# Grouped 32-column matmuls for router logits, layer-norm sums and step sizes, and turned sums moved between the last gate and up pieces

## What is computed

```python
# layer 0
z, xbc, dt, u, v = split(rmsnorm(x) @ W_in)          # 1024, 2048, 16, 1024, 1024 columns
xbc = silu(causal_conv4(xbc)); dt = softplus(dt + bias)
y = ssd(xbc, dt)                                     # 16 heads, state 64 x 128 per head
y = group_rmsnorm(y * silu(z))
g = gelu(u) * mix(layernorm(gelu(v)))                # spatial gating, chunks of 128 rows
x += concat(y, g) @ W_out;  x += swiglu(rmsnorm(x))  # D_FF = 2816
# layer 1
x += conformer_conv(rmsnorm(x))                      # GLU, 31-tap depthwise conv, layernorm, silu
logits = rmsnorm(x) @ router                         # 8 experts, the two largest are used
x += sum over the two experts e of gate_e * swiglu_e(rmsnorm(x))
return rmsnorm(x), new states
```

## Time and profile before

| | us |
|---|---|
| median of 3 runs | 1371.74 (1371.33 to 1373.18) |
| the profiled execution, its own time | 1371.72 |
| its span | 1370.0 |
| TensorE busy (matmul) | 1327.5, 97% of the span, 7031 instructions |
| VectorE (DVE) busy | 372.4, 27% |
| ScalarE (ACT) busy | 171.4, 13% |
| GpSimd (POOL) busy | 61.4, 4% |
| mean granted TensorE clock | 0.989 |
| DMA | 381.51 MB, mean 278 GB/s |

### The profile page before, as it was taken

One profiled execution on the slowest core, in us unless ns is written; L12 is line 12 of the kernel. 1 busy time (PEld: TensorE's weight loads), 2 busy tenths in 40 slices (PEclk: granted clock), 3 DMA queues, 4 the chain that ended last, 5 costly groups with the idle time before them and its releaser, 6 DMA issues.

```text
span 1370.0 us, 16556 instructions
## 1 busy us (share of the span) xinstructions
PE 1327.5 (97%) x7031; PEld 808.9 (59%) x7031; DVE 372.4 (27%) x829; ACT 171.4 (13%) x352; POOL 61.4 (4%) x87
## 2 busy tenths in 40 slices
PE   7999999999999999989999999999999999999887
PEld 6888888888888888858633335444333333333323
DVE  3535885421111115943310111100102011011011
ACT  1241423010000101032200000000000000000002
POOL 2003210000000202000000000000000000000000
PEclk9999999999999999999999999999999999999999
DMA  8537722565455433383799999996999999999994
GB/s 264 214 126 257 251 93 93 185 175 161 135 186 179 146 123 123 109 289 129 278 353 354 411 418 401 413 361 264 409 409 404 418 411 403 385 402 418 398 417 174
DMA packets 136155, 381.51 MB, mean 278 GB/s; under 512 B 6892, under 2 KB 62748, under 8 KB 129882
## 3 DMA queue, kind: packets, MB, share of 16 engines
q1 hardware_dynamic: 128339, 360.03, 69.7%
q0 software_dynamic: 3216, 11.54, 2.6%
q10 hardware_dynamic: 4530, 8.91, 2.0%
HBM read 372.54 MB, written 9.01 MB: 279 GB/s over the span
## 4 chain that ended last, share of the span: by engine, by line
PE 87%; DVE 5%; DMA 4%; SPq 1%; issue 1%; ACT 1%; DVEq 0%; ACTq 0%
PE ps L1730 30%; PE ps L2210 15%; PE ps L2281 13%; PE ps L2229 8%; PE ps L2241 4%; DVE both L1417 3%; PE ps L1956 3%; PE ps L2292 2%; DMA both<-in_moe_w_down_dram 2%; DMA both<-in_moe_w_gate_dram 2%; PE ps L2153 1%; PE ps L2258 1%; DMA both<-in_w_in_even_dram 1%; PE ps L1739 1%; PE ps L1948 1%; PE ps L2019 1%
## 5 line engine op out<-in xcount | busy, mean ns | idle before, releaser
L1730 PE MATMUL ps<-both 128*128 128x264 f32 x2080 | 472.4, 389 | 5.0 <-ACT both L978 3.7
L1730 PEld LDWEIGHTS ps<-both 128*128 128x128 f32 x2080 | 396.9, 192 | 75.1 <-issue 5.1
L2210 PE MATMUL ps<-both 128*64 128x512 f32 (+3 forms) x960 | 235.6, 563 | 8.3 <-DMA both<-in_moe_w_gate_dram 4.9
L2281 PE MATMUL ps<-both 128*64 128x512 f32 (+1 forms) x704 | 178.4, 597 | 1.9 <-DMA both<-in_moe_w_down_dram 1.9
L2210 PEld LDWEIGHTS ps<-both 128*64 128x64 f32 (+1 forms) x960 | 89.9, 148 | 137.9 <-issue 119.5
L2229 PE MATMUL ps<-both 128*64 128x512 f32 (+1 forms) x576 | 117.8, 560 | 0.9 <-ACT both L1007 0.9
L2281 PEld LDWEIGHTS ps<-both 128*64 128x64 f32 (+1 forms) x704 | 58.0, 143 | 101.8 <-issue 100.2
L2229 PEld LDWEIGHTS ps<-both 128*64 128x64 f32 x576 | 41.3, 137 | 68.4 <-issue 67.1
L1638 DVE TENSOR_TENSOR both<-both,ps 128x512 f32<-128x512 f32 (+1 forms) x18 | 16.7, 942 | 209.9 <-PE ps L2210 209.9
L2241 PE MATMUL ps<-both 128*32 128x512 f32 (+1 forms) x576 | 60.4, 560 | 0.0
L1627 DVE TENSOR_TENSOR both<-both,ps 128x512 f32<-128x512 f32 (+1 forms) x9 | 8.9, 987 | 132.6 <-PE ps L2229 132.6
(11 more groups left out here) (362 smaller groups left out, 904.4 us busy)
## 6 DMA issues: line engine op xcount, KB each, us to landing
both<-in_moe_w_up_dram SPq DMA_DIRECT2D x32, 2048.0 KB
both<-in_moe_w_gate_dram SPq DMA_DIRECT2D x32, 2048.0 KB
both<-in_moe_w_down_dram SPq DMA_DIRECT2D x32, 2048.0 KB
both<-in_moe_w_gate_dram SPq DMA_DIRECT2D x16, 1536.0 KB
both<-in_moe_w_down_dram SPq DMA_DIRECT2D x16, 1536.0 KB
both<-in_moe_w_up_dram SPq DMA_DIRECT2D x16, 1536.0 KB
both<-in_w_in_even_dram SPq DMA_DIRECT2D x10, 2048.0 KB
both<-in_ffn_w_gate_dram SPq DMA_DIRECT2D x11, 1024.0 KB
```

Of the source, the lines that this page charges most:

```text
L1730: ins = mm(ps[:, 0:T], w[:, c, cols:cols + P], src[:, c, :], start=c == 0, stop=c == nk - 1)
L2210: ins = mm(out, xg[:, 4 * j + c, 0:cap], w[:, c, r, :], start=j + c == 0, stop=j + c == 4)
L2281: ins = mm(out, lhsT, w[:, b - b0, 512 * h:512 * (h + 1)], start=b + r == 0, stop=b + r == 11)
```

## The change

Stationary blocks of 32 columns, put at output partitions 0, 32, 64 and 96 in turn (chunk c goes to group c mod 4), take the place of full-width ones, so that a tile holds four partial sums in its four quarters. A second, small matmul with stacked identities (mask32, 32 columns, each the sum of four identity blocks) or with ones joins the quarters.

- Step sizes: 8 grouped matmuls (tile dtp), copied by ScalarE into GV's first chunk, and, behind the turned conv rows, 3 joining matmuls into dt. Zeroed tails are added to wdt and wrt, as the last chunk's block reaches past them.
- The sample block moves from behind v3 to behind v1; ScalarE's copies and store with it, the broadcasts from behind v4's activation to behind v2's. dtT is no longer copied by ScalarE but multiplied by DVE into a block-diagonal matrix (dtown), and one matmul with odd spreads it. The matrices odd, own and mask32 are made by three reductions on DVE behind the x copies.
- Layer-norm sums of layer 0: `stat_part` (8 grouped) where `stat` was, a copy on ScalarE scaled by 1/32, `stat_joined` (1 matmul) one tile later; the root of the variance moves behind u5.
- Router logits: chunks 0 to 3 behind w2_5, 4 to 7 behind the norm's two sums; DVE copies tile lgp to SBUF; 3 joining matmuls behind three turned row groups.
- The last expert: (0,0), (0,1), (2,0) of the turned sums go between the pieces of `up(2, 10)`, (1,0) and (1,1) stay between those of `down(1, 14)`.

```diff
 psum_tiles
-    add("dt", ("dt_raw", 2))
+    add("dtp", ("dtp_ready", 1))
     for i in range(4):
         add(("crow", i), ("crow_ready", i + 1))
+    add("dt", ("dt_raw", 2))
     for c in range(DC):
         add(("v", c), ("gv_ready", c + 1))
-        if c == 3:
+        if c == 1:
...
         if i == 0:
-            add("lg", ("lg_ready", 2))
+            add("lgp", ("lgp_read", 1))
+    add("lg", ("lg_ready", 2))
 GpSimd
             then(g.memset(ident[:, :], 0.0))
+            then(g.memset(wdt[:, DC * 16:DC * 16 + 16], 0.0))
+            then(g.memset(wrt[:, DC * EXP:DC * EXP + 24], 0.0))
 ScalarE
+                if c == XBC:
+                    filled(act, "dtp")
+                    a.activation(dtp, tile("dtp")[:, 0:T], ACT.Copy).then_inc(sem("dtp_ready"), 1)
...
-                if c == 4:
+                if c == 2:
                     for k in range(4):
                         sample_bc(k)
-                if c == 3:
+                if c == 1:
...
-                    filled(act, "dtT")
-                    a.activation(dts[0:HEADS, :], tile("dtT")[0:HEADS, 0:16], ACT.Copy).then_inc(sem("dtT_ready"), 1)
...
+                if k in (1, 4):
+                    part = ("lnv_mean_part", "lnv_var_part")[k // 4]
+                    act.wait_ge(sem("stat_full"), STATS.index(part) + 1)
+                    a.activation(SQ1[:, 0, :], STAT[:, 0:T], ACT.Copy, scale=1.0 / 32).then_inc(sem("stat_read"), 1)
...
-                if k == 4:
+                if k == 5:
                     load_root_table()
                     root("lnv_var", 1)
 DVE
+            dve.wait_ge(sem("ident_ready"), 1)
+            then(v.tensor_reduce(mask32, ident[:, :].rearrange("p (d m) -> p m d", d=4), AX.X, ALU.add))
+            dve.wait_ge(sem("esel_ready"), 1)
+            then(v.tensor_reduce(odd, esel.rearrange("h c m -> h m c"), AX.X, ALU.add))
+            then(v.tensor_reduce(own, esel, AX.X, ALU.max))
...
+            filled(dve, "dtT")
+            v.tensor_tensor(dtown, bc(tile("dtT")[0:HEADS, 0:16], 1, [HEADS, DC, 16]), bc(own, 2, [HEADS, DC, 16]),
+                            ALU.mult).then_inc(sem("dtT_ready"), 1)
...
+            filled(dve, "lgp")
+            v.tensor_copy(lgs, tile("lgp")[:, 0:T]).then_inc(sem("lgp_read"), 1)
 TensorE
+            def stat_part(name, ready, SQ):
+
+                pe.wait_ge(sem("stat_read"), STATS.index(name))
+                for c in range(DC):
+                    g = 32 * (c % 4)
+                    pe.wait_ge(sem(ready), c + 1)
+                    ins = mm(STAT[g:g + 32, 0:T], ones[:, 0:32], SQ[:, c, :], start=c < 4, stop=c >= 4)
+                ins.then_inc(sem("stat_full"), 1)
+
+            def stat_joined(name, part):
+
+                pe.wait_ge(sem("stat_read"), STATS.index(name))
+                mm(STAT[:, 0:T], ones[:, :], part, start=True, stop=True).then_inc(sem("stat_full"), 1)
...
-            for k in range(BLK):
-                n = ROWS[k]
-                for c in range(DC):
-                    ins = mm(ps[0:n, 16 * k:16 * k + 16], H[:, c, P * k:P * k + n], wd[:, c, :], start=c == 0,
-                             stop=c == DC - 1)
+            for c in range(DC):
+                g = 32 * (c % 4)
+                ins = mm(ps[g:g + 32, 0:T], wdt[:, 16 * c:16 * c + 32], H[:, c, :], start=c < 4, stop=c >= 4)
...
+            pe.wait_ge(sem("dtp_ready"), 1)
+            ps = claim("dt")
+            for k in range(BLK):
+                n = ROWS[k]
+                ins = mm(ps[0:n, 16 * k:16 * k + 16], dtp[:, P * k:P * k + n], mask32[:, 0:HEADS], start=True,
+                         stop=True)
+            done(ins)
...
-                if s == 0:
+                    if s + j != 1 or s:
+                        continue
                     pe.wait_ge(sem("xc_ready"), XBC + 1)
...
-                    for c in range(DC):
-                        ins = mm(ps[:, 16 * c:16 * c + 16], esel[:, c, :], dts[0:HEADS, :], start=True, stop=True)
-                    done(ins)
+                    done(mm(ps[:, 0:P], odd, scr(10368, P)[0:HEADS, :], start=True, stop=True))
...
                     if s == 0 and j == 1:
-                        for c in range(DC):
-                            stat("lnv_mean", "gv_ready", 0, GV, c)
+                        stat_part("lnv_mean_part", "gv_ready", GV)
+                    if s == 0 and j == 2:
+                        stat_joined("lnv_mean", SQ1[:, 0, :])
                     if s == 1 and j == 0:
-                        for c in range(DC):
-                            stat("lnv_var", "vsq_ready", 0, SQ1, c)
+                        stat_part("lnv_var_part", "vsq_ready", SQ1)
+                    if s == 1 and j == 1:
+                        stat_joined("lnv_var", SQ1[:, 0, :])
...
 logits(c)
-                    pe.wait_ge(sem("lg_zero"), 1)
-                    mm(lg[:, 0:24], ident[:, :], L, start=True, stop=False)
                 pe.wait_ge(sem("h_ready"), 4 * DC + c + 1)
-                for k in (0, 1, 2) if c < DC - 1 else (1, 2, 0):
-                    n = ROWS[k]
-                    ins = mm(lg[0:n, 8 * k:8 * k + 8], H[:, c, P * k:P * k + n], wr[:, c, :], start=False,
-                             stop=k == 0 and c == DC - 1)
-                return ins
+                g = 32 * (c % 4)
+                return mm(lgp[g:g + 32, 0:T], wrt[:, EXP * c:EXP * c + 32], H[:, c, :], start=c < 4, stop=c >= 4)
...
-                    for c in range(3) if 4 * s + j == 3 else range(4 * s + j - 1, 4 * s + j) if 4 * s + j > 3 else ():
-                        logits(c)
+                    if 4 * s + j == 5:
+                        for c in range(4):
+                            logits(c)
...
-            ins = logits(DC - 1)
+            for c in range(4, DC):
+                ins = logits(c)
...
+            pe.wait_ge(sem("lgp_read"), 1)
+            ps = claim("lg")
+            for k in range(BLK):
+                n = ROWS[k]
+                ins = mm(ps[0:n, 8 * k:8 * k + 8], lgs[:, P * k:P * k + n], mask32[:, 0:EXP], start=True, stop=True)
+            done(ins)
...
 up(k, n, ...)
-                            if between and j + m == 0:
-                                between()
+                            if between:
+                                between(2 * j + m)
...
-                up(2, 10, 1, (lambda: scatter_block(3)) if s else None)
+                def between_up(i):
+
+                    if i == 0 and s:
+                        scatter_block(3)
+                    if s == STATIC and i == 1:
+                        pe.wait_ge(sem("moe_mul"), t * XMULS + (first + 2 * reps))
+                        pe.wait_ge(sem("t_free4"), t * STEP4 + (USES[s]["scat"][0] + SCAT))
+                        pe.wait_ge(sem("t_free5"), t * STEP5 + (USES[s]["scat"][1] + SCAT))
+                    if s == STATIC and i:
+                        sum_rows(*((0, 0), (0, 1), (2, 0))[i - 1])
...
                     if s == STATIC:
-                        if r == 1:
-                            pe.wait_ge(sem("t_free4"), t * STEP4 + (USES[s]["scat"][0] + SCAT))
-                            pe.wait_ge(sem("t_free5"), t * STEP5 + (USES[s]["scat"][1] + SCAT))
-                            for h in range(2):
-                                sum_rows(0, h)
-                        else:
-                            for h in range(2):
-                                sum_rows(1, h)
-                            sum_rows(2, 0)
-
+                        sum_rows(1, r - 1)
+
+                up(2, 10, 1, between_up)
                 down(1, 14, between_down)
```

More of the change, by code:

```diff
@@ L284, in build @@
         SQ0 = GV
+        dtp = GV[:, 0, :]
         st = reg(10608, 4096).rearrange("p (b c n) -> p b c n", b=4, c=DC)
@@ L326, in build @@
         SQ1 = scr(7168, DC * T).rearrange("p (c t) -> p c t", c=DC)
+        odd = scr(10240, P)[0:HEADS, :]
+        dtown = scr(10368, P)[0:HEADS, :].rearrange("h (c j) -> h c j", c=DC)
+        own = scr(10496, DC)[0:HEADS, :]
         esel = scr(11264, 1024)[0:HEADS, :].rearrange("h (c m) -> h c m", c=DC)
@@ L371, in build @@
         ysb = reg(11776, 1024)
+        lgs = ysb[:, 0:T]
         xg = reg(12800, 1024).rearrange("p (c j) -> p c j", c=DC)
@@ L472, in wview @@
             return ring[:, 4096 * slot:4096 * (slot + 1)] if n < NSM else ring[:, 6144 * slot:6144 * (slot + 1)]
-        wdt = sb("wdt", DC * 16)
-        wrt = sb("wrt", DC * EXP)
+        wdt = sb("wdt", DC * 16 + 16)
+        wrt = sb("wrt", DC * EXP + 24)
         bc = lambda ap, axis, shape: ap.unsqueeze(axis).broadcast_to(shape)
@@ L2029, in _ @@
                 stat("lnc_var", "csq_ready", 0, SQ2, c)
-            wr = wrt[:, :].rearrange("p (c n) -> p c n", c=DC)
-            lg = tile("lg")
+            lgp = tile("lgp")
             def logits(c):
                 if c == 0:
-                    for sname, value in TILES[NUM["lg"] - RING][1]:
+                    for sname, value in TILES[NUM["lgp"] - RING][1]:
```

(14 more changed lines are left out.)

10 lines of the change are left out of this document (4 added, 6 removed).

## The result

The changed kernel takes 1364.61 us (median of 4 runs, 1363.96 to 1366.13), the kernel before 1372.46 beside it (1371.33 to 1373.52): 0.9941 of its time, 95% interval 0.9925 to 0.9956. It is faster, inside the range, but 5.1 us over the forecast: 7.9 us were gained, not 12.2. The execution profiled took 1364.55 us, span 1362.8.

A forecast was written before the change was run, and what follows sets the result against it. TensorE, busy nearly the whole span, was taken to bound the kernel, with the chain on it wherever the change touches. Gains of 7.0, 2.3 and 2.9 sum to 12.2 us: 1371.7 - 12.2 = 1359.5 us, range 1356.0 to 1365.0.

The forecast's parts named there:

- Prices: On TensorE: a grouped block of eight 264-column matmuls costs 1.13 us instead of 3.56, of four 0.66, a join 0.445.
- the taps' row: Profile row of the conv taps in four column groups: 32 matmuls in 3.59 us, used to price the grouped blocks.
- Rival 4: Column groups don't overlap with one shared moving operand: each block of eight costs 3.56 us, total 1369.3; chance 0.04.
- Step sizes and the sample block: Ahead of the second v block: it starts at 98.0 us instead of 102.5, gain 4.5, whether the clock falls or not.
- Rival 1: Sample chain starts late, DVE only 4.5 us earlier; TensorE waits 2 to 3 before the variance: 1361.5 to 1362; chance 0.12.
- The two sums: Layer-norm mean and variance sums: 1.98 us less each on TensorE; spatial mix 7.0 us earlier, bounds 5.1 to 8.5.
- this chain is late next: Variance root, DVE's scaling of v and the running sums hold the spatial mix: gain 7.0 us instead of 8.5.
- Start additions: DVE's three reductions (some 2.7 us) and two tiny memsets fit DVE's idle stretch at the start: no cost.
- Router logits: Grouped logits between the last w2 tiles and the positions: 2.3 us gained before the experts, bounds 0.6 to 3.6.
- rival 2: The clock falls once or twice more in the new waits, 1.7 us per fall: 1361.2 to 1363; chance 0.15.
- Turned sums: Last expert: 12 turning matmuls move between gate and up pieces, hidden in DMA waits: 2.9 us gained, bounds 1.2 to 3.1.
- Rival 5: Weight stream from 1100 to 1339 us sets the end; at a rate 5.1% lower the 12.2 us are gone; chance 0.02.

## Why the prediction was right, and where it failed

**Prices.** Right in sum: a grouped block of eight took 1.10 us in each place. From start to start, with what the full-width tile behind it takes over 3.56, that is 1.14 for the mean's sum (127.61 to 128.64, then 3.67 to 132.31), forecast 1.13; the join 0.44 (132.31 to 132.75), forecast 0.445; the logits' first four 0.69 (633.12 to 640.93 less two tiles), forecast 0.66. The sum was right by some luck: the block itself took 1.03 where the taps' row gave 0.93, and the change of form and back 0.11 where the forecast had 0.2. The rule of the Trainium skill that was weighed ("TensorE: Matmul & The Clock Gate", "Measured speedup vs the span model", 2.38 times for three tiles) would have made each block 0.2 longer, by an estimate from its figure. Its rate gives 1.11 for the block, the taps' 0.93, and the 1.03 measured lies between; the taps' row with the forecast's 0.2 came nearer for block and change together. Rival 4, no overlap, is out.

**Step sizes and the sample block.** Right: second v block at 98.93, that is 98.0 and the 1.0 of the late end of xbc. The clock held between 86 and 92 (1.00 where it was 0.72), and by the wait for the decay that was worth nothing, as forecast. Rival 1 did not come: DVE took the mean at 133.02, having waited 1.11 us for the join, and TensorE does not wait before the variance.

**The two sums.** Right in size and in cause. From the end of xbc to the mix 6.7 and 6.6 us, forecast 7.0, and "this chain is late next" is what the run with the whole variance sum shows: DVE's scaling of v holds the mix, and the second of the two splits is worth 0.4 us of its 1.98.

**Start additions.** Put at nothing, and no cost shows: at the end of xbc the nine profiles with them are 0.2 us earlier in the mean than the four without, with a scatter of over 2 us in either group.

**Router logits.** This is the step that failed: "2.3 us in front of the experts", with bounds 0.6 to 3.6, measured at -1.8. Its times up to the clock's fall were right: the last w2 tile 9.0 us earlier by the profile (5.4 carried and 3.6 its own); the logits in DVE at 644.97 against 652.79, 5.4 + 2.4 where 2.3 was forecast; and the fifth row turn waited for ScalarE, as said. What it had wrong is the price of that wait. The wait was 2.08 us long at the end of a chain of very small matmuls, and the clock fell in it. The forecast had priced such a fall at 1.7 us, from 6 us of mixed work in the earlier trace rows, and put it in rival 2 with 0.15; in the sum it stood at nothing. The clock was low for nearly 14 us, over the last row turns, the positions and most of the gather: the stretch got 1.8 us longer instead of 2.3 shorter, and the first expert's first piece came 3.6 us earlier instead of 9.3.

By the spans 5.0 us are missing (7.2 for 12.2): 4.1 here, 1.0 by the late end of xbc, 0.3 between there and the mix and 0.4 between mix and w2, less 0.7 more than forecast in the last expert, rounded. Three things show that most of the 4.1 went to the clock: the logits of before bring the stretch back to 52.5; the five idle matmuls cut it by 5.3 us (6.9 of the whole by medians); and with all waits filled the same edit gives 1.8 us in the stretch and 2.2 in the whole. Not all of the 5.3 is the change's own, since filling the waits of the kernel before gives 1.6 in the same stretch. The change's own loss to the clock is therefore 3.7 us, or 3.6 by the pair with all fillers (1.8 for -1.8); the other 0.5 is the term itself, 1.8 for the 2.3 forecast. So the term was about right for its work, and rival 2's price was half of what one such fall cost.

The rule of the Trainium skill named in rival 2, that transposes don't count for the clock ("TensorE: Matmul & The Clock Gate", "Part 4: PE-mode transpose"), was not what decided: the turned rows ahead of the mix held 1.00 again in the changed kernel (154 to 160, TensorE busy 4.89 of 6 us); what fell was a stretch whose longest part was a wait.

**Turned sums.** Right: 2.9 us forecast, 2.9 alone on the kernel before (2.6 by its stage), 3.3 to 3.6 in the profiles with the rest. Rival 5, the weight stream, did not come: 401 GB/s from 1100 to 1220 and 411 from 1280 to 1339, before 400 and 409.

Not settled: why the clock falls behind a wait in one execution and not in another (the 1.31 us ahead of the gather, the 1.20 for the decay), and whether it is the idle time or the lack of long matmuls that does it. No run changed the start alone either; the ends of xbc speak against a cost there, but could hide a few tenths.

## What to carry to other kernels

Column groups are worth their price in the profile (eight fp32 blocks of 32 columns in 1.10 us, not 3.56), but work taken from TensorE ahead of a wait for another engine lengthens the wait, and a lengthened wait among small matmuls can cost again behind it, through the granted clock (here 3.6 us). Before a change that empties TensorE's queue, look at the granted clock behind the nearest waits and price a fall over all the small-matmul work that follows. Where such a wait can't be removed, idle matmuls into a free bank may be the cheapest edit: here 32 of them, in four waits of 1.3 to 3.7 us, took 9.8 us off the changed kernel (1364.61 to 1354.86, medians of two series), more than the change itself had gained (7.9). Compare two kernels with the clock kept in both, since part of that gain was to be had in the kernel before as well (6.3).

## What was unexpected of the hardware

- **The clock stayed low while TensorE was busy.** In the changed kernel it was 0.50 from 648 to 660 us, though TensorE was busy 3.75, 2.69 and 4.00 us of each 4. It was back at 1.00 from 661 us, nearly 6 us into the gather. In three of the four profiles with the five fillers the same work ran at 1.00 throughout; in the fourth it fell in the gather.
- **The gather's length is the clock's.** The same 48 instructions took 5.57 us at 1.00, 7.20 with a fall part of the way, and 8.36 at 0.50 for most of it.
- **A fall is not certain.** Behind the same wait of 1.31 us ahead of the gather the clock held in one profile with the five fillers and fell in another.
